# Hybrid decoder layer on 8 cores: the last product in two halves, and one of the last four scalings on other engines

## What is computed

```python
y = jnp.concatenate([rmsnorm(ya, g_a), rmsnorm(yb, g_b), rmsnorm(yc, g_c)], axis=-1)
out = jnp.einsum('bse,ed->bsd', y, w_out[l])
x = x + rmsnorm(out, norm_post[l])
```

## Time and profile before

| | |
|---|---|
| median of 3 runs | 1285.12 us |
| the runs | 1285.12, 1285.99, 1257.85 us |
| the profiled execution | 1259.11 us |
| its slowest core's span (core 6) | 1257.5 us |
| spans of the others | 1253.1 to 1256.8 us |
| TensorE busy on core 6 | 1216.6 us (97%) |
| VectorE, ScalarE, GpSimd busy | 533.4, 442.2, 164.1 us |

### The profile page before, as it was taken

One profiled execution on the slowest core, in us unless ns is written; L12 is line 12 of the kernel. 1 busy time (PEld: TensorE's weight loads), 2 busy tenths in 40 slices (PEclk: granted clock), 3 DMA queues, 4 the chain that ended last, 5 costly groups with the idle time before them and its releaser, 6 DMA issues.

```text
span 1257.5 us, 17343 instructions; the slowest of 8 cores (1253.1 to 1257.5 us)
## 1 busy us (share of the span) xinstructions
PE 1216.6 (97%) x6088; PEld 574.1 (46%) x6210; DVE 533.4 (42%) x896; ACT 442.2 (35%) x811; POOL 164.1 (13%) x208
## 2 busy tenths in 40 slices
PE   4999999999999999999999999999999999999996
PEld 1444455444444444444444444444444444434443
DVE  2686664456444444443222233232233237222366
ACT  3566622223555455553222222222232222222222
POOL 0000221101011111111001010101010112112021
PEclk9999999999999999999999999999999999999999
DMA  8974399320313040304005249947282669994299
GB/s 194 207 226 134 53 163 155 60 41 3 65 43 62 1 68 1 67 2 67 1 1 84 50 67 179 159 65 129 45 158 38 101 101 153 155 161 60 42 176 259
DMA packets 32757, 119.39 MB, mean 95 GB/s; under 512 B 3296, under 2 KB 9696, under 8 KB 29024
## 3 DMA queue, kind: packets, MB, share of 16 engines
q0 software_dynamic: 22480, 76.03, 38.1%
q1 hardware_dynamic: 10192, 42.25, 13.2%
HBM read 164.93 MB, written 29.36 MB: 155 GB/s over the span
## 4 chain that ended last, share of the span: by engine, by line
PE 90%; DMA 5%; DVE 2%; issue 2%; ACT 1%; SPq 0%; DVEq 0%; POOL 0%; ACTq 0%; POOLq 0%
PE ps L382 89%; DMA arena<-wst 4%; DMA arena<-xT 1%; PE ps L965 1%; DVE arena L479 0%; DVE arena L1258 0%; DVE arena L639 0%; DVE arena L1225 0%; DVE arena L645 0%; PE ps L562 0%; SPq L386 0%; DVE arena L1293 0%; DVE arena L660 0%; ACT L593 0%; ACT arena L612 0%
## 5 line engine op out<-in xcount | busy, mean ns | idle before, releaser
L382 PE MATMUL ps<-arena 128*128 128x512 bf16 (+3 forms) x5800 | 1210.9, 367 | 31.3 <-ACT arena L453 14.4
L382 PEld LDWEIGHTS ps<-arena 128*128 128x128 bf16 x5922 | 561.1, 98 | 665.2 <-issue 42.6
L1225 DVE SCALAR_TENSOR_TENSOR arena<-ps,arena 128x512 f32<-128x512 f32 x128 | 95.7, 750 | 165.4 <-PE ps L382 161.7
L537 ACT ACTIVATE arena<-arena 128x512 bf16<-128x512 f32 x96 | 68.8, 716 | 248.0 <-DVE arena L1114 173.7
L1229 ACT ACTIVATE ps<-arena 128x512 f32<-128x512 f32 x64 | 38.5, 601 | 222.9 <-PE ps L382 144.9
L389 POOL DMA_DIRECT2D arena<-wst x120 | 66.8, 571 | 329.2 <-PE ps L382 299.8
L1108 DVE SCALAR_TENSOR_TENSOR arena<-ps,arena 128x512 f32<-128x512 f32 x32 | 24.0, 751 | 155.4 <-PE ps L382 63.8
L555 POOL TENSOR_TENSOR arena<-arena 128x512 bf16<-128x512 bf16 x28 | 34.7, 1240 | 366.4 <-ACT arena L540 273.1
L593 ACT ACTIVATE arena<-ps 128x512 f32<-128x512 f32 x60 | 35.2, 596 | 125.2 <-PE ps L382 125.0
L639 DVE TENSOR_TENSOR arena<-arena 128x514 f32<-128x514 f32 (+5 forms) x72 | 55.2, 766 | 50.2 <-ACT arena L612 45.2
L540 ACT ACTIVATE arena<-arena 128x512 bf16<-128x512 f32 x96 | 58.8, 613 | 0.0
(11 more groups left out here) (78 smaller groups left out, 425.5 us busy)
## 6 DMA issues: line engine op xcount, KB each, us to landing
arena<-wst POOLq DMA_DIRECT2D x120, 512.0 KB, 13.5
arena<-xT SPq DMA_DIRECT2D x16, 1024.0 KB, 11.3
out<-arena POOLq DMA_DIRECT2D x12, 1024.0 KB, 14.9
arena<-x SPq DMA_DIRECT2D x4, 1024.0 KB, 17.9
out<-arena SPq DMA_DIRECT2D x16, 256.0 KB, 9.1
arena<-memT SPq DMA_DIRECT2D x2, 1024.0 KB, 6.1
arena<-norm_post SPq DMA_DIRECT2D x1, 1024.0 KB, 9.8
arena<-poolw_l POOLq DMA_DIRECT2D x1, 512.0 KB, 7.6
```

The source lines that it names most:

```text
L382: return lambda e: e.matmul(out, lhsT=lhsT, rhs=rhs, start=start, stop=stop)
L537: P.op("act", lambda e: e.activation(out=yT[:, c, tb * 512:(tb + 1) * 512], in_=tmp[ti][:], func=AF.Copy, scale=cp[:, CP_GBR + c:CP_GBR + ...
L1225: P.op("dve", lambda e: e.scalar_tensor_tensor(out=ra, in0=pv, scalar=sc(c), in1=ra, op0=ALU.mult, op1=ALU.add), reads=[bk(b), ("rbr", br) ...
```

## The change

The last product (tile 8 of the second half, block 3, branch 1) is made in two halves of 256 columns (last_mm), each with 8 matmuls into a bank of its own. Each half has its own eviction on VectorE and its own squares with a sum on ScalarE (last_evict); the first half's sum is added on VectorE to what head_sum had made, and the second's goes into the root in queue_x. The product with gpost stays on VectorE, in a bank that is set aside once, before the stage. In this unit one quarter of the tile before is emitted already after branch 0, so ahead of branch 2's eviction. Of the last tile's quarters, 1 and 2 stay on VectorE; then quarter_side does quarter 0 with a scaling on ScalarE and an addition of x on GpSimd; then comes quarter 3 on VectorE. The stores are issued in that order: 1, 2, 0, 3.

```diff
--- before.py
+++ after.py
@@ -348,6 +348,7 @@
     ST_SO = 136
     ST_FO = 200
     ST_FR = 216
+    ST_LAST = 232
 
 
     use = {b: 0 for b in range(1, 8)}
@@ -1209,7 +1210,37 @@
                            for k in ks],
                     reads=[M_ytile(br * 8, t), M_wo(s, hf)], writes=[bk(b)])
 
-    tail = []
+    tail = bank()
+
+    def last_mm():
+        i = ordr[8]
+        t, s = tok_of(1, i), o_slot[23]
+        for h in range(2):
+            b = bank()
+            obank[h] = b
+            for hf in range(2):
+                P.group("pe", [mm(psb(b, 0, 256), yT[:, 8 + k, t * 128:(t + 1) * 128],
+                                  wo[s][:, k, h * 256:h * 256 + 256], k == 0, k == 7)
+                               for k in range(hf * 4, hf * 4 + 4)],
+                        reads=[M_ytile(8, t), M_wo(s, hf)], writes=[bk(b)])
+
+    def last_evict():
+        i = ordr[8]
+        t = tok_of(1, i)
+        for h in range(2):
+            b, ra = obank[h], rows[i][:, 3, h * 256:h * 256 + 256]
+            Mr, so = Mem((o_row[i] + 6 * KB + h * KB, KB)), (ST_SO + t * 4 + 3, ST_LAST)[h]
+            P.op("dve", lambda e, b=b, ra=ra: e.scalar_tensor_tensor(
+                out=ra, in0=psb(b, 0, 256), scalar=sc(ST_RBR + 16 + t), in1=ra, op0=ALU.mult, op1=ALU.add),
+                reads=[bk(b), ("rbr", 1), Mr], writes=[Mr])
+            P.op("act", lambda e, b=b, ra=ra, so=so: e.activation(out=psb(b, 0, 256), in_=ra, func=AF.Square,
+                                                                  accum_out=sc(so)),
+                 reads=[Mr], writes=[bk(b), ("so", t, 3 + h)])
+        P.op("dve", lambda e: e.scalar_tensor_tensor(
+            out=sc(ST_FO + t), in0=sc(ST_SO + t * 4 + 3), scalar=1.0 / D, in1=sc(ST_FO + t), op0=ALU.mult,
+            op1=ALU.add), reads=[("so", t, 3), ("fo", t)], writes=[("fo", t)])
+        P.op("dve", lambda e: e.tensor_tensor(out=psb(tail), in0=rows[i][:, 3, :], in1=gpost[:, 1536:2048],
+                                              op=ALU.mult), reads=[row_M(i, 3), M_gp], writes=[bk(tail)])
 
     def o_evict(half, db, i, br):
         t = tok_of(half, i)
@@ -1229,12 +1260,7 @@
             P.op("act", lambda e: e.activation(out=asrow(i, psb(b)), in_=ra, func=AF.Square,
                                                accum_out=sc(ST_SO + t * 4 + db)),
                  reads=[row_M(i, db)], writes=[bk(b), ("so", t, db)])
-            if xadd and i == ordr[8] and db == 3:
-                bl = bank()
-                tail.append(bl)
-                P.op("dve", lambda e: e.tensor_tensor(out=psb(bl), in0=ra, in1=gpost[:, 1536:2048], op=ALU.mult),
-                     reads=[row_M(i, db), M_gp], writes=[bk(bl)])
-            elif xadd:
+            if xadd:
                 P.op("pool", lambda e: e.tensor_tensor(out=ra, in0=ra, in1=gpost[:, db * 512:(db + 1) * 512],
                                                        op=ALU.mult),
                      reads=[row_M(i, db), M_gp], writes=[row_M(i, db)])
@@ -1271,7 +1297,7 @@
         dma_sp(row_full(j), asrow(j, x_d[t * 128:(t + 1) * 128, :]),
                writes=[row_M(j, db) for db in range(4)], sem=f"d_xr{j}")
 
-    fq = []
+    fq, late_q = [], []
 
     def fill(n):
         for _ in range(min(n, len(fq))):
@@ -1282,6 +1308,15 @@
              reads=[("so", t, db) for db in range(3)], writes=[("fo", t)])
         P.op("dve", lambda e: e.tensor_scalar(out=sc(ST_FO + t), in0=sc(ST_FO + t), scalar1=1.0 / D, scalar2=EPS,
                                               op0=ALU.mult, op1=ALU.add), reads=[("fo", t)], writes=[("fo", t)])
+
+    def quarter_side(i, db):
+        t = tok_of(1, i)
+        av, xr = rows[i][:, db, :], row_ap(xrow[i], db)
+        P.op("act", lambda e: e.activation(out=av, in_=av, func=AF.Identity, scale=sc(ST_FR + t)),
+             reads=[("fr", t), row_M(i, db)], writes=[row_M(i, db)])
+        P.op("pool", lambda e: e.tensor_tensor(out=av, in0=av, in1=xr, op=ALU.add),
+             reads=[row_M(i, db), row_M(xrow[i], db)], writes=[row_M(i, db)])
+        dma_sp(out_d[t * 128:(t + 1) * 128, db * 512:db * 512 + 512], av, reads=[row_M(i, db)], sem=f"d_ox{i}{db}")
 
     def quarter(i, db):
         t = tok_of(1, i)
@@ -1289,7 +1324,7 @@
         av, xr = rows[i][:, db, :], row_ap(j, db)
         if j >= 7:
             av = av.rearrange("p (a b) -> p a b", b=256)
-        src, Ms = (psb(tail[0]), bk(tail[0])) if i == ordr[8] and db == 3 else (av, row_M(i, db))
+        src, Ms = (psb(tail), bk(tail)) if i == ordr[8] and db == 3 else (av, row_M(i, db))
         P.op("dve", lambda e: e.scalar_tensor_tensor(
             out=av, in0=src, scalar=sc(ST_FR + t), in1=xr, op0=ALU.mult, op1=ALU.add),
             reads=[("fr", t), Ms, row_M(j, db)], writes=[row_M(i, db)])
@@ -1298,13 +1333,17 @@
 
     def queue_x(i):
         t = tok_of(1, i)
-        P.op("act", lambda e: e.activation(out=sc(ST_FR + t), in_=sc(ST_SO + t * 4 + 3), func=AF.Sqrt,
+        c, k = (ST_LAST, 4) if i == ordr[8] else (ST_SO + t * 4 + 3, 3)
+        P.op("act", lambda e: e.activation(out=sc(ST_FR + t), in_=sc(c), func=AF.Sqrt,
                                            bias=sc(ST_FO + t), scale=1.0 / D),
-             reads=[("so", t, 3), ("fo", t)], writes=[("fr", t)])
+             reads=[("so", t, k), ("fo", t)], writes=[("fr", t)])
         P.op("dve", lambda e: e.reciprocal(out=sc(ST_FR + t), in_=sc(ST_FR + t)), reads=[("fr", t)],
              writes=[("fr", t)])
-        for db in range(4):
+        last = i == ordr[8]
+        for db in range(1 if last else 0, 4):
             fq.append(lambda db=db: quarter(i, db))
+        if last:
+            late_q.append(lambda: quarter_side(i, 0))
 
     def unit(half, db, i):
         for br in BRO:
@@ -1360,7 +1399,15 @@
         i = ordr[p]
         if p >= 5 and db == 3:
             head_sum(tok_of(1, i))
-        unit(1, db, i)
+        if p == 8 and db == 3:
+            for br in (0, 2):
+                o_mm(1, 3, i, br)
+                o_evict(1, 3, i, br)
+                fill(1)
+            last_mm()
+            last_evict()
+        else:
+            unit(1, db, i)
         fill(2)
         if p >= 5 and db == 3:
             queue_x(i)
@@ -1369,7 +1416,9 @@
             if q < 4:
                 load_xrow(ordr[q + 5], ordr[q])
         pend = [p] if db == 3 and p < 5 else []
-    fill(4)
+    fill(2)
+    late_q.pop()()
+    fill(2)
     P.finish("d_out", "d_ox")
 
     sem_names = sorted(P.count.keys())
```

## The result

The changed kernel is slower: its time is 1.0029 times that of the kernel before, 95% interval 1.0017 to 1.0041, some 3.6 us. The forecast was no change: 1259.1 us for an execution like the profiled one, own range 1258.8 to 1259.4. That execution took 1262.23 us. (The medians over all 12 executions of each, 1272.26 us before and 1265.57 after, mix in executions in which the cores of a die ran at a lower clock; the ratio is over the others.)

A forecast was written before the change was run, and what follows sets the result against it. It took the end of the slowest core, 6, to be bound by a line of stores: last landing unchanged at 1257.2, span 1257.5, plus 1.6 around the span, giving 1259.1 us, own range 1258.8 to 1259.4.

The forecast's parts named there:

- the sum: Adding up the end: last issue -0.5 to +0.4 us on core 6, landing 1257.2 unchanged, span 1257.5, execution 1259.1.
- the line of stores: At core 6's end, queued stores set the landing at 1257.2, whatever the last issue time, if before 1254.9.
- GpSimd's addition: In last-tile quarter 0: 1.26 us alone, ending 1252.6 at best, or about 1253.3 if waiting for VectorE's second quarter.
- Rival 2: Shared reads at the end: last issue 0.8 us later, deciding past 1254.9; 1259.5 to 1260.3 us; chance 0.15.
- Rival 1: Core 6's end follows the chain, so an earlier issue ends earlier: 1258.3 to 1258.6 us; chance 0.22.
- Rival 3: Last product: first eviction waits for both halves; 0.4 us on core 0's chain, nothing on core 6; 1259.1; chance 0.04.
- The moved quarter: Before the last branch's eviction, VectorE does the same two operations in the other order: worth 0.
- The two halves: Last product: matmuls cost 0, evictions 0.48 us each; with the squares, first quarter 0.07 earlier on core 6, 0.26 on core 0.
- the squares: On ScalarE after the last eviction: 0.42 us for the second half's 256 columns instead of 0.60 for 512, -0.19.
- the one-column sum and the product: On VectorE beside ScalarE's squares and root: below 0.2 us and 0.75 at most, costing the chain 0.
- the 217 GB/s: Core 6's DMA rate between 1250 and 1252, at a share of 0.95; read as part still working off older stores.

The follow-up runs named there:

- e5: Kernel before with only the quarter of the tile before moved ahead of branch 2's eviction in the last unit; ratio to the kernel before 0.9998.
- e6: Kernel before with only the last product in two halves, all four quarters on VectorE, none moved; ratio to the kernel before 1.0003.
- e7: Kernel before with the halves, all quarters on VectorE, and quarters that waited for their row of x emitted one unit later; ratio to the kernel before 0.9998.
- e2: Kernel before with only the last tile's quarter 0 done by ScalarE and GpSimd, stores 1, 2, 0, 3; ratio to the kernel before 1.0012.
- e3: Kernel before plus a one-column GpSimd memset waiting for a last-tile quarter: late (quarter 3) ratio 1.0017, early (quarter 0) 1.0004, to the kernel before.
- e4: Changed kernel with the moved quarter back behind branch 2's eviction, halves and GpSimd addition kept; ratio to the kernel before 1.0025.
- e1: Changed kernel with quarter 0 of the last tile on VectorE again, everything else as changed; ratio to the kernel before 0.9996.

## Why the prediction was wrong

**The step that failed is the sum.** It took the span's end as the last landing plus 0.3 us, on every core ("core 6 by the line of stores, 1257.2, unchanged"). That holds in the kernel before, where GpSimd's last instruction came 11 us before the end of core 6. The 0.3 us were read, but not what they consist of: the engines meet at the end, and each comes with a DRAIN of its own. The row of it stood in the trace of the kernel before, 6967 ns on GpSimd's queue, ending 4 us before the landing. The prediction priced GpSimd's addition by its 1.26 us and by what waits for its data (SyncE's queue). It did not ask what the last instruction on an engine's list carries behind it. With that row the sum would have been, on core 6: addition from 1252.0 to 1253.3, plus 5.57, plus 0.2, is 1259.1 instead of 1257.5, +1.6 us, and on core 0 about 1259.6: slower, beyond all of the cases given (core 0's execution would be 1261.2, the slowest case was 1260.3). Rival 2 had the right sign and the wrong mechanism: its threshold, 1254.9 for the last issue, was computed for the stores. Core 6 did pass it, with 1255.4, and as computed the landing then followed the issue, by 2.4 us. But that accounts for only 0.5 us of this core's 3.2; the other 2.7 are the DRAIN. Rival 1 expected a faster kernel and none was seen. Rival 3 is refuted by core 4, where the first half is evicted before TensorE's end.

**GpSimd's addition.** On the data side it went as costed. It began 0.9 us after the first quarter (0.7 in the sum) and took 1.62: that is 0.36 us more than the 1.26 of a product alone. The second quarter, which had begun first, is the likely reason; no run has an addition on GpSimd alone. The last store left 3.0 us after the first quarter, within the stated 2.4 to 3.3.

**The moved quarter was costed at nothing, and that was wrong in its mechanism.** The sum said "the same two operations before the last branch's eviction, only in the other order". The order decides who stands beside GpSimd's product: an eviction with one SBUF operand loses nothing, a quarter with two loses 0.65 us. The prediction used exactly this effect for the new addition and did not look for it at the moved step. The Trainium skill (SBUF — State Buffer, section "SBUF: two separate sides") has the later of the two block fully. The trace agrees for most of it: the quarter began at 1247.79, GpSimd's product ended at 1248.64, and of these 0.85 us the quarter lost 0.65. On core 6 this excess and a wait of 0.17 us between two evictions, which the quarter had covered, go into VectorE's lateness, and since the DRAIN follows the addition, into the span's end. Without GpSimd at the end it costs nothing measurable (e5).

**The two halves.** The form measured 0.48 us as worked out from the neighbouring sizes, the squares 0.38 (0.42 expected). On cores in time the first quarter came 0.42 us earlier. The sum had 0.26 for core 0, since it took VectorE to be behind there; on five of eight cores it was not. On core 6 the gain was nearly nil (2.35 us from the first eviction to the first quarter, 2.37 before), where 0.07 was expected. The cost of 0 for the one-column sum and the product held: the sum waited 0.38 us for the first half's squares and the product came only at 1251.37, but the reciprocal began 0.10 us after the root had ended, as before. The missing 0.05 us lie on ScalarE, where the root starts 0.33 us after the read of the accumulator does, before 0.28; no run says why.

**The line of stores.** This reading holds as far as it was tested. Last issues from 4.87 to 5.53 us gave last landings between 7.1 and 11.3 on cores in time, with no order in them, and e6, with the last store 0.43 us earlier, and e7, with all cores in time, gained no time. That one engine of the 16 is the slowest is still only argued from the landings and the 217 GB/s.

**The size.** On cores in time the end moved from a median of 9.44 to 10.39, +0.95 us. On the slowest, core 6, VectorE was also 2.2 us late, and the DRAIN carried that along: landing seen at 1257.8, end at 1260.7. Before, the stores' line hid such lateness up to about 1.7 to 2.1 us. This is an estimate: a last landing at 9.2 to 9.6, less the 5.2 us from the last eviction's start to the last issue, less 2.3 us of landing. Now nothing hides it. That gives 1 to 3 us by core, and 3.6 (2.1 to 5.2) measured.

**Where the lateness comes from** can be read from the waits. On every late core VectorE has stood still once, until 8 to 12 us before TensorE's end, in front of a quarter whose row of x had not arrived. On core 6 this took 4.2 us before (the line is under e7) and 4.7 after (total us, times, longest):

```profile
DVE arena L1328 <- DMA arena<-x: 4.7, 1, 4.7
```

The profiles other than e7's have 36 cores whose last eviction starts more than the usual 0.11 us after TensorE's end. On all of them the delay is this wait less a constant, within 0.02 us: 3.78 in the order of before (also e2, e3), 3.41 with the halves (e4, e6), 2.95 with the moved quarter (e5), 2.57 with both (after, e1). So for the same wait the change makes a late core 1.2 us later. The halves cost 0.4 of that, since the last eviction is now the second of two, and give as much back behind it (1.95 us from it to the first quarter instead of 2.37). The moved quarter costs 0.8, its 0.65 and the gap of 0.17. On core 6, with this wait of 4.7, the order of before would still have been 0.9 us late; the change made it 2.2.

**What stays open.** Why the row of x came later on some cores and in some executions (the waits of late cores go from 2.8 to 7.0 us). Whether halves or moved quarter add to the time of the GpSimd addition: 1.0012, 1.0025 and 1.0029 have intervals that overlap. And why GpSimd's DRAIN takes 5.57 us: it does so behind an addition, a product and a memset alike, but this kernel issues 133 transfers from GpSimd's queue, and no run was made without them.

## What to carry to other kernels

Before giving the last instructions of a kernel to an engine that has been idle, look at how its list closes: the DRAIN rows on the line that opens the block, each against the last landing. An idle engine is not free to use there if its end is expensive. Here GpSimd had to be finished about 5.5 us before the last store lands (5.57, less the 0.07 until SyncE has seen the landing). Any instruction later than that, even a memset of one column, moves the end of its core one for one: in e3's late run 5.57 us and the meeting of 0.23 stand behind the memset on all eight cores.

And when an operation is moved, look at who runs beside its new place, not only at what it waits for and what waits for it.

## What the runs showed of the hardware

GpSimd's closing DRAIN ends 5.57 us after its last instruction, whichever that is: 6.97 us in all behind a product of 1.37 to 1.38, 7.22 behind an addition of 1.62, 5.68 behind a memset of 0.10. VectorE's took 1.95 to 2.59 us and ScalarE's 0.31 to 0.73, but these end 0.05 and 0.04 us after the last instruction of their engine. SyncE's took 0.007 to 0.013. The Trainium skill (VectorE: DVE Perf Modes, section "The DRAIN you can't avoid") gives the runtime's DRAINs, before and behind a kernel, as about 12 ns on all engines. SyncE's agrees; for the one that closes GpSimd's list here the measurement decides, 5.68 to 7.22 us.

A quarter, a VectorE operation with two SBUF operands, beside GpSimd's product: 0.74 became 1.39 to 1.40 us in four kernels (after, e1, e5, e7). An eviction, with one operand in PSUM, stayed at 0.75 there.
